# Leaving out, for the context tokens of a two-block transformer layer, the columns and results that only latent tokens use

## The chip, the cores and the metric

The kernel runs on one core of a Trainium2 chip. The number that counts is the device time of one execution in microseconds (us), the median over runs. Engines are called PE (TensorE matmul; PEld is its weight load), DVE (VectorE), ACT (ScalarE), POOL (GpSimd) and SP (SyncE, here a queue that only issues DMAs).

## The reference, cut to what matters

Two blocks run one after the other on 1,024 latent tokens of width 1,024. The change touches the first third of the first block, its token mix. That block has 256 context tokens beside the latent ones, but its depth is 1, so `need_ctx` is false and no output of a context token leaves it:

```python
u, uc = h @ w_in, hc @ w_in                     # 1024 and 256 tokens, 4544 columns
q, k, v, gf, gb = split_heads(u)                # retention, 5 x 512 columns
yc_f, sc_f = retention_scan(qc, kc, vc, log_gamma, s0)   # yc_f is not used, sc_f is
y_f, _ = retention_scan(q, k, v, log_gamma, sc_f)
r, w_f, w_b, k, v, a, b, g_f, g_b, bonus = rwkv_prepare(rw, ...)    # rwkv, 1984 columns
yc_f, sc_f = rwkv7_scan(rc, wc_f, kc, vc, ac, bc, s0)    # again only the state sc_f is used
y_f, _ = rwkv7_scan(r, w_f, k, v, a, b, sc_f)
if not need_ctx:
    return lat, None
```

The context serves for the two groups' states alone: of its retention part q and the two gates gf, gb are not used, and of its rwkv part the receptance r, the output gates and the per-token results.

## The kernel before

The program is a row of stages. Each stage is a block with its own buffers and semaphores, and the next begins when all engines and the queues of the last are done. Inside a stage every engine has its own written order of instructions with waits on semaphores; nothing is moved by a scheduler. Tokens stand context first: columns 0 to 255 of every transposed array are context (TC = 256), 256 to 1279 latent. P is 128, BANK is 512 columns of one PSUM bank.

**proj1** (`gemm_T`) writes `uT`, the 4,544 projected columns as rows, for 1,280 tokens. It has G = 18 groups of 256 columns (the last has 192). A group is two halves e of 128 columns (the last one 64), and each half three token chunks of 512, 512 and 256, each 8 x 3 matmuls (k tiles times hi x hi, lo x hi, hi x lo of a split product) into its own bank. ACT splits the next weights (`leading`, L527) and drains half 0 (L517); DVE makes the rest of the weights (`rest`, L548), drains half 1 (L517) and adds up the modulation vectors that later stages need (`piece`, L562); SP loads weights two groups ahead (L436), stores a half when it is drained (L468), and loads the pieces (L446).

**ret** (`retention`) loads q, k, v of 128 rows at a time (L665); only the latent part of q is read by any instruction. Its first work on DVE needs the table `ax`, loaded behind the first q and k.

**prep** (`rwkv_prepare`) goes over 12 units, four row pairs p times three token parts c: c = 0 is the 256 context tokens, c = 1 and 2 are 512 latent tokens each. In step i PE widens a norm for unit i - 3 (L1190), makes unit i's three convolutions k, v, r (`conv`, L1150), its low-rank products (L1164, L1166) and its norm sums (L1177), and for a latent unit i - 3 the gates (L1200) and the bonus sum (L1207). ACT takes the convolutions out of PSUM (L1254) between its exponentials (L1276 to L1278); DVE runs `rates`, `keys`, `results` of unit i - 3, the last of which multiplies r into one of four stored arrays (L1392, semaphore o1) and for latent units makes the bonus (L1397). POOL copies a few columns of the exponentials (`wcol`, L1125), for which L1392 waits, and after a context unit builds the nine diagonal matrices of the pair after next (L1103).

**chunks** (`rwkv_chunks`) takes 40 steps q, one for each pair and block of 128 tokens; 8 of them are context (the first two blocks of each pair's ten). A step inverts two triangular matrices by 5 levels of products in turn with ACT and DVE: `t1` on PE (L1541), a copy on ACT, `pp` on PE (L1551), a predicated copy on DVE (L1798). Between these PE does other work, among it for the step before: `results` (L1569, L1573, L1577; two blocks of 12 matmuls, in level 2 behind `pp` and in level 4 behind `t1`) and `states` (L1589 and on). DVE and ACT bring the results out (`res` L1811, `yis` L1711) beside the chunk matrices `mt`, `nn`. SP stores `res` and `yis` and loads the block four steps ahead, in a loop with registers. The next stage reads only the latent blocks of what was stored.

## Time and profile before

| | |
|---|---|
| median of 3 runs | 4752.97 us (4750.97 to 4757.22) |
| profiled execution, span | 4752.7 us |
| PE busy | 4004.5 us, 84% |
| DVE busy | 2760.1 us, 58% |
| ACT busy | 2047.4 us, 43% |
| stages that the change touches | 57 to 1500 us of the span |
| behind them, untouched | 1500 to 4752.7 us |

The profiled execution's own time is its span, 4752.7 us, 0.3 us under the median of the runs; a sum made in the span can be laid on the median as it is. A matmul record's length is pipelined (records overlap), so the time that a run of matmuls takes is read from start to start. Float32 matmuls stand in the trace as two records each, those on the split fp32r operands as one.

### The profile page before, as it was taken

To read this page: it belongs to the slowest core of one execution; us is meant where nothing else is said; L and a number is where in the kernel's file an instruction comes from. 1 tells how busy PE (TensorE), PEld (TensorE's weight loads), DVE (VectorE), ACT (ScalarE), POOL (GpSimd) and SP (SyncE) were. 2 spreads that over 40 slices of the span, in tenths; PEclk is the share of its full clock that TensorE was granted. 3 is DMA by queue.
4 is the path that set the end of the run, shared out by engine and by line. 5 is a ranking of instruction groups with operands and counts; after the bars stand their busy time and mean duration, and the time that the engine had idled before them with its cause. 6 is when DMAs were issued, how large, how long until landed. Compare 5 with 4: busy or idle time off the path is not lost. (4 is left out here: it accounts for less than half of the span.)

```text
span 4752.7 us, 76279 instructions
## 1 busy us (share of the span) xinstructions
PE 4004.5 (84%) x31217; PEld 3199.8 (67%) x31217; DVE 2760.1 (58%) x4042; ACT 2047.4 (43%) x3461; POOL 470.8 (10%) x376
## 2 busy tenths in 40 slices
PE   6999976878887675999939889699989896499994
PEld 4888744448886454888838767477777664388883
DVE  4222155566665558999951476455543354599995
ACT  3111022545553324777731344355532232377772
POOL 0000012210001200111010132000000000111111
PEclk9999966979999787999969999899999898699997
DMA  5332221652223445999942232322133304699996
GB/s 203 133 133 99 79 99 53 176 166 80 78 80 112 143 178 200 395 398 390 377 150 93 92 113 85 105 71 75 55 109 104 113 28 179 251 409 413 410 413 249
DMA packets 378959, 842.33 MB, mean 177 GB/s; under 512 B 32703, under 2 KB 249823, under 8 KB 328182
## 3 DMA queue, kind: packets, MB, share of 16 engines
q1 hardware_dynamic: 360526, 787.44, 45.2%
q0 software_dynamic: 12032, 41.96, 2.8%
q10 hardware_dynamic: 6056, 8.08, 0.5%
q8 instruction: 249, 4.08, 0.4%
q14 instruction: 96, 0.79, 0.1%
HBM read 673.03 MB, written 164.35 MB: 176 GB/s over the span
## 5 line engine op out<-in xcount | busy, mean ns | idle before, releaser
L506 PE MATMUL psum<-proj_hi,proj_w 128*128 128x512 f32 (+2 forms) x1728 | 461.8, 356 | 13.1 <-DVE proj_w L548 11.4
L4443 DVE TENSOR_TENSOR moe_lo<-moe_raw,moe_hi 128x2048 fp32r<-128x2048 f32 x192 | 428.4, 2286 | 33.6 <-ACT moe_hi L4398 33.6
L4398 ACT ACTIVATE moe_hi<-moe_raw 128x2048 fp32r<-128x2048 f32 x192 | 357.0, 1911 | 40.9 <-PE psum L4359 40.9
L506 PEld LDWEIGHTS psum<-proj_hi,proj_w 128*128 128x128 f32 (+1 forms) x1728 | 303.9, 188 | 66.6 <-DVE proj_w L548 11.6
L506 PE MATMUL psum<-proj_lo,proj_w 128*128 128x512 f32 (+2 forms) x864 | 306.2, 354 | 0.0
L517 DVE COPY proj_out<-psum 128x512 f32<-128x512 f32 (+3 forms) x54 | 32.5, 603 | 355.6 <-PE psum L506 355.6
L2738 DVE TENSOR_TENSOR moe_lo<-ahead_raw,moe_hi 128x2048 fp32r<-128x2048 f32 x96 | 219.1, 2290 | 23.5 <-ACT moe_hi L2686 23.4
L2738 DVE TENSOR_TENSOR moe_lo<-lT,moe_hi 128x2048 fp32r<-128x2048 f32 x96 | 218.9, 2290 | 21.9 <-ACT moe_hi L2686 21.9
L2686 ACT ACTIVATE moe_hi<-ahead_raw 128x2048 fp32r<-128x2048 f32 x96 | 184.2, 1919 | 70.9 <-PE psum L2639 70.9
L2686 ACT ACTIVATE moe_hi<-lT 128x2048 fp32r<-128x2048 f32 x96 | 183.9, 1919 | 66.3 <-PE psum L2639 66.3
L1798 DVE COPY_PREDICATED chunks_X<-chunks_msk,psum 128x128 f32<-128x128 int32 x400 | 107.8, 302 | 152.3 <-PE psum L1551 138.0
L1711 ACT ACTIVATE chunks_T<-psum 128x128 f32<-128x128 f32 x400 | 102.9, 278 | 206.3 <-PE psum L1541 202.0
L506 PEld LDWEIGHTS psum<-proj_lo,proj_w 128*128 128x128 f32 (+1 forms) x864 | 162.4, 188 | 23.9
L4359 PE MATMUL psum<-moe_hi,moe_xh 128*128 128x512 f32 x512 | 165.6, 405 | 9.8 <-DVE moe_lo L4443 9.8
L3387 PE MATMUL psum<-h_hi,g_w 128*128 128x512 f32 x512 | 169.1, 412 | 0.0
L506 PE MATMUL psum<-h_hi,proj_lru_w 128*128 128x512 f32 x512 | 159.2, 392 | 11.7 <-DVE proj_lru_w L548 11.7
L2639 PE MATMUL psum<-moe_hi,moe_xh 128*128 128x512 f32 x512 | 162.0, 398 | 4.9 <-DVE moe_lo L2738 4.9
L3487 DVE TENSOR_REDUCE attn_nmax<-psum 128x1 f32<-128x256 f32 (+7 forms) x128 | 90.9, 752 | 128.8 <-PE psum L3339 128.8
L4359 PE MATMUL psum<-moe_hi,moe_xl 128*128 128x512 f32 x512 | 160.5, 395 | 0.0
L4359 PE MATMUL psum<-moe_lo,moe_xh 128*128 128x512 f32 x512 | 159.7, 393 | 0.0
L2639 PE MATMUL psum<-moe_hi,moe_xl 128*128 128x512 f32 x512 | 159.1, 392 | 0.0
L2639 PE MATMUL psum<-moe_lo,moe_xh 128*128 128x512 f32 x512 | 159.0, 392 | 0.0
(647 smaller groups left out, 9940.2 us busy)
## 6 DMA issues: line engine op xcount, KB each, us to landing
moe_raw<-in_w_gate_up SPq DMA_DIRECT2D x128, 1024.0 KB, 9.6
moe_raw<-in_w_down SPq DMA_DIRECT2D x64, 1024.0 KB, 7.8
lT<-in_w_gate SPq DMA_DIRECT2D x36, 1024.0 KB, 9.3
ahead_raw<-in_w_down SPq DMA_DIRECT2D x36, 1024.0 KB, 8.0
ahead_raw<-in_w_up SPq DMA_DIRECT2D x32, 1024.0 KB, 10.1
lT<-in_w_up SPq DMA_DIRECT2D x32, 1024.0 KB, 9.7
ahead_raw<-in_w_gate SPq DMA_DIRECT2D x28, 1024.0 KB, 8.9
lT<-in_w_down SPq DMA_DIRECT2D x28, 1024.0 KB, 7.9
```

What stands on the lines that cost most here:

```text
L506: ins = nc.tensor.matmul(bank[e * nch + c][0:width, 0:n], l, r, start=(k == 0 and i == 0), stop=(k == KD - 1 and i == 2))
L517: ins = nc.scalar.activation(o, i, ACT.Copy) if e == 0 else nc.vector.tensor_copy(o, i)
L1711: nc.scalar.activation(dst, src, ACT.Copy).then_inc(s[sem], 1)
L1798: nc.vector.copy_predicated(X[:, j, g, :, c], msk[:, g, 1 + l, :, c], Lb[g][:, P:3 * P].rearrange("p (h t) -> p h t", h=2)[:, :, c])\
L2639: last = nc.tensor.matmul(out[c][:, :], x[:, k, :], w[:, n % R, i, c * BANK:(c + 1) * BANK], start=(k == 0 and m == 0), stop=(k == KD - 1 ...
L2686: nc.scalar.activation(hi[:, n % R], raw(n), ACT.Copy).then_inc(s["hi_ready"], 1)
L2738: nc.vector.tensor_tensor(lo[:, n % R], raw(n), hi[:, n % R], ALU.subtract).then_inc(s["lo_ready"], 1)
L3387: ins = nc.tensor.matmul(bank[7][:, :], g_w[:, c % 2, l, k, :], h_part[r][:, k, b * BANK:(b + 1) * BANK], start=(k == 0 and i == 0), stop= ...
L3487: nc.vector.tensor_reduce(nmax[:, j, m:m + 1], psum[:, at(j, m):at(j, m) + n], AX_X, ALU.max, negate=True)\
L4359: last = nc.tensor.matmul(out[c][:, :], x[:, k, :], w[:, n % R, i, c * BANK:(c + 1) * BANK], start=(k == 0 and m == 0), stop=(k == last_k ...
L4398: nc.scalar.activation(hi[:, n % R], raw[:, n % RAW], ACT.Copy).then_inc(s["hi_ready"], 1)
L4443: nc.vector.tensor_tensor(lo[:, n % R], raw[:, n % RAW], hi[:, n % R], ALU.subtract).then_inc(s["lo_ready"], 1)
```

## The change

In the projection nine of the 18 groups start at token 256 (`NO_CONTEXT`): groups 0, 1 (retention q), 6 to 9 (retention gates), 10, 11 (r) and 17 (the tail of the output gates' low-rank columns). They have two token chunks of 512 instead of three; every count of semaphores goes by `before[g]`, the chunks of the groups ahead. The retention stage loads q from column 256. In prep a context unit loads no r, has no r convolution, no copy of it and no product o1 (the bare exponential is stored in its place, and is not used); the waits that hung on these go by the latent units alone. In chunks a context step has no `results` matmuls, no `res` and `yis`, and no stores, and SP's loop is written out.

```diff
+NO_CONTEXT = (0, 1, 6, 7, 8, 9, 10, 11, 17)
...
+    begin = [TC if g in late else 0 for g in range(G)]
+    chunks = [[(a, min(BANK, tok - a)) for a in range(begin[g], tok, BANK)] for g in range(G)]
+    before = [sum(len(chunks[j]) for j in range(g)) for g in range(G + 1)]
...
-                        sp.wait_ge(ev[e], nch * (g + 1))
-                        sp.dma_start(dst[g * GW + e * P:g * GW + e * P + size[g][e], :], ob[0:size[g][e], e, :]).then_inc(stored[e], 16)
+                        sp.wait_ge(ev[e], before[g + 1])
+                        sp.dma_start(dst[g * GW + e * P:g * GW + e * P + size[g][e], begin[g]:tok], ob[0:size[g][e], e, begin[g]:tok])\
+                            .then_inc(stored[e], 16)
...
-                            pe.wait_ge(ev[e], nch * g)
+                            pe.wait_ge(ev[e], before[g])
                         width = size[g][e]
-                        for c, (a, n) in enumerate(chunks):
+                        for c, (a, n) in enumerate(chunks[g]):
...
-                        sp.dma_start(t[:, b, :], uT[p * P + a:p * P + a + P, :]).then_inc(loaded[b], 16)
+                        first = TC if t is q else 0
+                        sp.dma_start(t[:, b, first:], uT[p * P + a:p * P + a + P, first:]).then_inc(loaded[b], 16)
...
+        def streams(n):
+            return "kvr" if latent(n) else "kv"
...
-                    for k in range(2):
+                    for k in range(0 if latent(n) else 1, 2):
...
-                        sp.wait_ge(done, n + 1)
+                        if done is s["o1"]:
+                            sp.wait_ge(s["exps"], 3 * n + 3)
+                            sp.wait_ge(done, lat(n + 1))
+                        else:
+                            sp.wait_ge(done, n + 1)
...
-                    for which in "kvr":
+                    for which in streams(n):
...
-                        act.wait_ge(s["o1"], n - R + 1)
+                        act.wait_ge(s["o3"], n - R + 1)
+                        act.wait_ge(s["o1"], lat(n - R + 1))
...
-                        conv_out(i, "r")
+                        if latent(i):
+                            conv_out(i, "r")
...
-                    nc.vector.tensor_tensor(e[:, 0, :, 0:m], e[:, 0, :, 0:m], both(un[:, 0, 0:m]), ALU.mult).then_inc(s["o1"], 1)
+                    if latent(n):
+                        dve.wait_ge(s["ring_ev"], ring_at["r", n] + 1)
+                        nc.vector.tensor_tensor(e[:, 0, :, 0:m], e[:, 0, :, 0:m], both(un[:, 0, 0:m]), ALU.mult).then_inc(s["o1"], 1)
...
+        def latent(q):
+            return q % NBK >= NTC
...
-                    sp.sem_inc(s["turns"], 1)
-                    for dst, src in ((re, res), (yi, yis)):
+                    for dst, src in ((re, res), (yi, yis)) if latent(q) else ():
...
-                with sp.Fori(0, Q // R - 1) as it:
-                    for j in range(R):
-                        store(it * R + j)
-                        load(it * R + (R + j), j)
+                for q in range(Q):
+                    store(q)
+                    if q + R < Q:
+                        load(q + R)
...
+                    if not latent(q):
+                        return
                     four(out_a)
                     four(out_v)
                     four(out_v2)
...
-                        nc.vector.tensor_tensor(res[:, :, c, :], b[:, 0], pr[:, j, 1:4:2, half[c]], ALU.add).then_inc(s["c_dve"], 1)
+                        if latent(q):
+                            nc.vector.tensor_tensor(res[:, :, c, :], b[:, 0], pr[:, j, 1:4:2, half[c]], ALU.add).then_inc(s["c_dve"], 1)
```

Nothing is put in another order; instructions fall out of the engines' orders. In chunks, this is PE's order in step 1, from `pp` of level 2 to `pp` of level 3 (L1541 is `t1`, L1551 and L1553 `pp`, L1512 and L1514 the transposes of the step after, L1569 to L1577 `results` of step 0, a context block). Before:

```order
L1551 MATMUL psum<-chunks_T,chunks_X 64x64 x8
L1569 MATMUL psum<-chunks_LL,chunks_TT 64x64 x4
L1573 MATMUL psum<-chunks_LL,chunks_TT 64x64 x4
L1577 MATMUL psum<-chunks_LL,chunks_vrow 64x64 x4
L1541 MATMUL psum<-chunks_X,chunks_LL 64x64 x8
L1512 MATMUL psum<-cst,chunks_pr 128x128 x3
L1514 MATMUL psum<-cst,chunks_vt 128x128
L1512 MATMUL psum<-cst,chunks_pr 128x128 x3
L1551 MATMUL psum<-chunks_T,chunks_X 64x64 x8
```

And in the changed kernel (L1579 is `pp`, L1569 now `t1`, L1540 and L1542 the transposes):

```order
L1579 MATMUL psum<-chunks_T,chunks_X 64x64 x8
L1569 MATMUL psum<-chunks_X,chunks_LL 64x64 x8
L1540 MATMUL psum<-cst,chunks_pr 128x128 x3
L1542 MATMUL psum<-cst,chunks_vt 128x128
L1540 MATMUL psum<-cst,chunks_pr 128x128 x3
L1579 MATMUL psum<-chunks_T,chunks_X 64x64 x8
```

The 12 matmuls of `results` between `pp` and `t1` are gone; the second 12, between `t1` and `pp` of level 4, go in the same way.

In prep, this is PE's order around the second context convolution (unit 3), before:

```order
L1190 MATMUL psum<-prep_rs,prep_spread 128x128 x2
L1150 MATMUL psum<-prep_rin,prep_dg 128x256 x9
L1164 MATMUL psum<-prep_wl,prep_w2t 128x256 x2
L1166 MATMUL psum<-prep_al,prep_a2t 128x256
L1177 MATMUL psum<-prep_sqk,prep_zsel 32x128 x2
L1190 MATMUL psum<-prep_rs,prep_spread 128x128 x4
L1150 MATMUL psum<-prep_rin,prep_dg 128x512 x9
```

And in the changed kernel:

```order
L1209 MATMUL psum<-prep_rs,prep_spread 128x128 x2
L1169 MATMUL psum<-prep_rin,prep_dg 128x256 x6
L1183 MATMUL psum<-prep_wl,prep_w2t 128x256 x2
L1185 MATMUL psum<-prep_al,prep_a2t 128x256
L1196 MATMUL psum<-prep_sqk,prep_zsel 32x128 x2
L1209 MATMUL psum<-prep_rs,prep_spread 128x128 x4
L1169 MATMUL psum<-prep_rin,prep_dg 128x512 x9
```

The context convolution has six matmuls for nine, and everything behind it on PE stands as before.

## Rows read from the trace of the kernel before

**Rows 1.** The page's first line and its engines.

```profile
span 4752.7 us, 76279 instructions
```

**Rows 2.** Busy time by window: us; PE, PEld, DVE, ACT, POOL; clock, DMA.

```profile
57.00:582.00 525.00, 508.22 (x2614) 427.32 (x2612) 133.04 (x130) 73.36 (x85) 0.00 (x0) 0.99 0.33 112
582.00:811.00 229.00, 170.54 (x1200) 110.02 (x1200) 114.23 (x248) 60.05 (x163) 29.85 (x12) 0.68 0.20 72
811.00:1027.00 216.00, 162.46 (x496) 85.30 (x496) 142.40 (x186) 111.49 (x174) 62.59 (x82) 0.83 0.67 191
1027.00:1500.00 473.00, 407.40 (x13080) 386.81 (x13080) 285.22 (x1120) 231.62 (x999) 41.53 (x40) 0.97 0.29 79
```

**Rows 3.** Waits, window 57 to 585: total us, times, longest.

```profile
DVE proj_out L517 <- PE psum L506: 355.6, 54, 18.9
```

**Rows 4.** Timeline of PE, group 0: start us, us, what.

```profile
85.02 0.40 PE L506 MATMUL psum<-proj_hi,proj_w 128*128 128x256 f32 x2
87.89 0.63 PE L506 MATMUL psum<-proj_hi,proj_w 128*128 128x512 f32 x2
```

**Rows 5.** Timelines of ACT and SP, groups 7, 8; landings of proj_raw.

```profile
298.86 1.92 ACT L527 ACTIVATE proj_w<-proj_raw 128x2048 fp32r<-128x2048 f32 x1 [13.46 <-PE psum L506]
326.41 1.91 ACT L527 ACTIVATE proj_w<-proj_raw 128x2048 fp32r<-128x2048 f32 x1 [13.45 <-PE psum L506]
...
308.81 0.38 SPq L436 DMA_DIRECT2D proj_raw<-in_w_in  x1
...
DMA to landing us min/median/max: 5.3/7.2/11.0
```

**Rows 6.** Tile ret_q; timeline of DVE at the start of ret.

```profile
L665 SPq DMA_DIRECT2D ret_q<-uT x4: 319/324/432, 582.6 to 695.8; - x4
...
591.74 0.69 DVE L886 TENSOR_TENSOR ret_tmp<-psum,ret_ax 128x512 f32<-128x512 f32 x1 [12.94 <-DMA ret_ax<-in_ax]
```

**Rows 7.** Timeline of PE in prep, steps 6 and 7; one window.

```profile
904.51 6.54 PE L1150 MATMUL psum<-prep_rin,prep_dg 128*128 128x256 f32 x18
913.68 8.00 PE L1150 MATMUL psum<-prep_rin,prep_dg 128*128 128x512 f32 x18
...
905.00:910.00 5.00, 5.00 (x14) 3.96 (x14) 0.77 (x3) 0.95 (x3) 0.00 (x0) 0.56 0.45 142
```

**Rows 8.** Timelines of PE and ACT at the start of prep.

```profile
825.67 6.70 PE L1150 MATMUL psum<-prep_rin,prep_dg 128*128 128x256 f32 x18 [17.70 <-POOL prep_dg L1103]
...
830.36 1.28 ACT L1298 ACTIVATE prep_wl<-prep_wl 128x1282 f32<-128x1282 f32 x1 [24.57 <-issue]
```

**Rows 9.** Timelines of DVE and POOL in prep, units 3, 4 and 7.

```profile
914.27 0.78 DVE L1392 TENSOR_TENSOR prep_ex<-prep_ex,prep_u 128x512 f32<-128x512 f32 x1
926.30 1.22 DVE L1392 TENSOR_TENSOR prep_ex<-prep_ex,prep_u 128x1024 f32<-128x1024 f32 x1 [0.77 <-POOL wcol L1125]
971.45 0.69 DVE L1397 TENSOR_TENSOR prep_gt<-psum,prep_u 128x512 f32<-128x512 f32 x1 [0.88 <-PE psum L1207]
...
914.14 11.78 POOL L1103 TENSOR_SCALAR prep_dg<-cst,prep_pcs 128x128 f32<-128x128 f32 x9
```

**Rows 10.** Timeline of PE in chunks, step 0.

```profile
1047.22 0.63 PE L1551 MATMUL psum<-chunks_T,chunks_X 64*64 64x64 f32 x16
1048.02 0.68 PE L1541 MATMUL psum<-chunks_X,chunks_LL 64*64 64x64 f32 x16 [0.17 <-DVE chunks_X L1798]
1050.40 0.68 PE L1541 MATMUL psum<-chunks_X,chunks_LL 64*64 64x64 f32 x16 [0.17 <-DVE chunks_X L1798]
1051.22 0.68 PE L1553 MATMUL psum<-chunks_X,chunks_T 64*64 64x64 f32 x16
```

**Rows 11.** Timeline of PE in chunks, a later step.

```profile
1128.90 0.34 PE L1597 MATMUL psum<-chunks_vrow,chunks_rows 64*64 64x64 f32 x7 [1.67 <-issue]
1133.90 0.56 PE L1551 MATMUL psum<-chunks_T,chunks_X 64*64 64x64 f32 x13
1134.74 0.68 PE L1541 MATMUL psum<-chunks_X,chunks_LL 64*64 64x64 f32 x16
```

More of the change, by code:

```diff
@@ L396, in turn, with gemm_T @@
         return (KD * v + KD - 1) // self.PER + 2
-def gemm_T(nc, bank, name, actT, tok, w, col0, widths, dst, later=None, split=None):
+def gemm_T(nc, bank, name, actT, tok, w, col0, widths, dst, later=None, split=None, late=()):
     full, last = widths
-    chunks = [(a, min(BANK, tok - a)) for a in range(0, tok, BANK)]
-    nch = len(chunks)
+    nch = (tok + BANK - 1) // BANK
     GW = 2 * P
@@ L513, in drain @@
                 width = size[g][e]
-                for c, (a, n) in enumerate(chunks):
-                    eng.wait_ge(mm[e], g * nch + c + 1)
+                for c, (a, n) in enumerate(chunks[g]):
+                    eng.wait_ge(mm[e], before[g] + c + 1)
                     o, i = ob[0:width, e, a:a + n], bank[e * nch + c][0:width, 0:n]
@@ L525, in leading @@
                     if g >= 2:
-                        act.wait_ge(mm[1], nch * (g - 1))
+                        act.wait_ge(mm[1], before[g - 1])
                     nc.scalar.activation(wt[:, g % 2, 0, :, 0:n], raw[:, g % 2, :, 0:n], ACT.Copy).then_inc(hi_ready, 1)
@@ L546, in rest @@
                     if g >= 2:
-                        dve.wait_ge(mm[1], nch * (g - 1))
+                        dve.wait_ge(mm[1], before[g - 1])
                     nc.vector.tensor_tensor(wt[:, g % 2, 1, :, 0:n], raw[:, g % 2, :, 0:n], wt[:, g % 2, 0, :, 0:n], ALU.subtract)\
@@ L1039, in pc @@
             return pcs[:, p, PCOL[name] + i:PCOL[name] + i + 1]
+        def streams(n):
+            return "kvr" if latent(n) else "kv"
         ring_at = {}
         for n in range(STEPS):
-            for k in range(3 if n < UNITS else 0):
-                ring_at["kvr"[k], n] = len(ring_at)
+            for which in streams(n) if n < UNITS else "":
+                ring_at[which, n] = len(ring_at)
             for d in range(2 if n >= NP and latent(n - NP) else 0):
@@ L1088, in _ @@
                     if n < UNITS - NP:
-                        sp.wait_ge(s["ring_mm"], ring_at["r", n] + 1)
+                        sp.wait_ge(s["ring_mm"], ring_at[streams(n)[-1], n] + 1)
                         load_unit(n + NP)
@@ L1141, in conv @@
                     p, c, a, m = unit(n)
-                    pe.wait_ge(rin_in[c], 64 * (p + 1))
+                    pe.wait_ge(rin_in[c], (64 if latent(n) else 48) * (p + 1))
                     if n == 0:
@@ L1439, in rwkv_chunks @@
         names = ("tab_in", "tr", "rows_ev", "g_mm", "ll", "x_id", "x_one", "x_tr", "lakv_mm", "lakv_ev", "t1_mm", "t1_ev",
-                 "p_mm", "x_ev", "x_turned", "ta_mm", "ta_ev", "y_mm", "c_dve", "c_act", "stored", "turns")
+                 "p_mm", "x_ev", "x_turned", "ta_mm", "ta_ev", "y_mm", "c_dve", "c_act", "stored")
         s = {n: st.sem(n) for n in names}
@@ L1447, in rwkv_chunks @@
         PER_IN = 16 * 2
+        def latent(q):
+            return q % NBK >= NTC
+        c_dve = [sum(4 if latent(t) else 2 for t in range(q)) for q in range(Q + 1)]
+        c_act = [sum(6 if latent(t) else 4 for t in range(q)) for q in range(Q + 1)]
+        stored = [sum(32 if latent(t) else 0 for t in range(q)) for q in range(Q + 1)]
         def each_step(step):
@@ L1668, in out0 @@
                             if evac:
-                                after("c_act", q * 6 - 6)
+                                after("c_act", c_act[q - 1])
                             results(q - 1, jp, 0)
@@ L1738, in out @@
                 def out(q, j, c):
-                    act.wait_ge(s["c_dve"], q * 4 + (2 * c + 2))
-                    if c == 0:
-                        act.wait_ge(s["stored"], q * 32 + 1)
-                    copy(yis[:, :, c, :], Cb[c][:, P:2 * P].rearrange("p (d t) -> p d t", d=2), "c_act")
+                    act.wait_ge(s["c_dve"], c_dve[q] + (c + 1) * (2 if latent(q) else 1))
+                    if latent(q):
+                        if c == 0 and stored[q]:
+                            act.wait_ge(s["stored"], stored[q])
+                        copy(yis[:, :, c, :], Cb[c][:, P:2 * P].rearrange("p (d t) -> p d t", d=2), "c_act")
                     for d in range(2):
@@ L1807, in out @@
                     dve.wait_ge(s["y_mm"], q + 1)
-                    dve.wait_ge(s["stored"], q * 32 + 1)
+                    if latent(q) and stored[q]:
+                        dve.wait_ge(s["stored"], stored[q])
                     for c in range(2):
                         b = Cb[c][:, :].rearrange("p (w d t) -> p w d t", w=4, d=2)
-                        nc.vector.tensor_tensor(res[:, :, c, :], b[:, 0], pr[:, j, 1:4:2, half[c]], ALU.add).then_inc(s["c_dve"], 1)
+                        if latent(q):
+                            nc.vector.tensor_tensor(res[:, :, c, :], b[:, 0], pr[:, j, 1:4:2, half[c]], ALU.add).then_inc(s["c_dve"], 1)
                         nc.vector.tensor_tensor(mt[:, :, 2 * (q % NBK) + c, q // NBK, :], b[:, 2], idc.unsqueeze(1).to_broadcast([P, 2, H]), ALU.add)\
@@ L4554, in program @@
                 [(cst[:, :], tabs["cst"]), (col[:, :], tabs["cols"])], sc, x["ctx"][0], x["x"][0], hT)
-        gemm_T(nc, bank, "proj1", hT, TT, x["w_in"][0], 0, (D_IN // 512 * 2, ((P, P), (P, 64))), uT,
+        gemm_T(nc, bank, "proj1", hT, TT, x["w_in"][0], 0, (D_IN // 512 * 2, ((P, P), (P, 64))), uT, late=NO_CONTEXT,
                later=Later(x["w_mod"], x["b_mod"], x["norm_gains"], sc, cst[:, CONST["ones"]:CONST["ones"] + 1], mod))
```

22 lines of the change are left out of this document (10 added, 12 removed).

## The prediction

> **What bounds the kernel now.** I read the span cut at the stages first. The profiled execution took 4752.7 us [rows 1]; the change touches four stages, from 57 to 1500 us, and what lies behind is not edited. The reader is to see in the windows that each stage has a limit of its own: in proj1 PE is busy 508 of 525 us, at a granted clock of 0.99 of full speed (the 2.4 GHz level); in ret and prep PE's clock is at 0.68 and 0.83 and no engine is full; in chunks PE is busy 407 of 473 us [rows 2].
>
> For proj1 the view of waits comes next. DVE waits there for PE before all of its 54 drains, 356 us in all [rows 3], and ACT waits 13.5 us for it before each weight split [rows 5]. So the stage is PE's matmuls, one behind the other, and a matmul left out is time won as long as weights and drains keep up.
>
> For ret I read what its first DVE work waits for: the table `ax` [rows 6]. For prep and chunks the shares of busy time say little, since engines wait for each other by turns; there I went through the timelines of all engines over one pair and over one step, and asked at each removed instruction which wait ends last behind it.
>
> **proj1.** In group 0, the 24 matmuls of 128x256 of one half run from 85.02 to 87.89, 2.87 us [rows 4]; the next half's 512-wide ones begin at once. A late group loses two such chunks, 5.74 us, and there are nine late groups: 9 x 5.74 = 51.7. Against it goes that the last half has 64 weight columns, so that its chunk may be a little shorter, and that the last drain before the stage's end is now 512 wide instead of 256; 0.4 us for both is an estimate. I take **-51.3**.
>
> Do weights keep up? The load for group 10 is issued at 308.81 and lands 7.2 us later in the median, 11.0 at worst, while ACT can't begin to split before group 8 ends, at 326.41 [rows 5]. That leaves 10.4 us, 6.6 at worst; a late group takes 5.74 of it. Even a load behind that would have a whole group more, since group 9 runs in between. DVE has 356 / 54 = 6.6 us to spare before each drain, its splits, pieces and sums included [rows 3]. So nothing new is waited for; this term's bounds are -50 and -52.
>
> **ret.** q, k and `ax` are 640, 640 and 1024 KB, issued from 582.6, and DVE starts when `ax` has landed at 591.74 [rows 6]: 2304 KB in 9.1 us, 0.5 us for the 128 KB that q loses. Later loads are early. **-0.4**, bounds 0 and -0.6.
>
> **prep.** A context unit loses 3 of 9 convolution matmuls on PE, one copy on ACT and one product on DVE. On PE, 18 records of 512 take 8.00 us at the high level, 0.444 each, so six of 256 are 1.33 us; the nine of a context unit took 6.54, as they begin behind a wait with the clock at 0.56, and a third of that is 2.18 [rows 7]. The r matmuls are the last three, when the clock has risen, so I take 1.33. On DVE L1392 costs 0.6 to 0.7 us of its queue [rows 9]. Whether that counts must be asked for each of the four context units:
>
> - Start: PE runs units 0 to 2 without a gap and DVE waits for the end of that. But behind the shorter convolution PE needs the tanh that ACT ends at 830.36 + 1.28 = 831.64 [rows 8], and 825.67 + 6.70 - 1.33 is 831.04. So 0.7 to 0.8 of the 1.33 is had.
> - Pairs 0 and 1: DVE comes 0.7 us sooner to the next unit, and at its L1392 waits for `wcol`, which POOL copies behind nine diagonals that start at 914.14 and take 11.78, to 925.9 [rows 9]. These start by ACT's exponentials, which the change doesn't move. The gain ends there: 0.
> - Pair 2 (no diagonals follow): DVE waits 0.88 us at L1397 for PE's bonus sum [rows 9]. DVE's 0.7 and PE's 1.33 both come through: 1.3.
> - Pair 3: DVE runs on without a wait, 0.6.
>
> Sum **-2.7**. Bounds: 0, and 4 x (1.33 + 0.6) = -7.7 if both engines' savings added up each time.
>
> **chunks.** Eight context steps lose twice 12 matmuls (24 records). Do these cost time? In a later step the block between `pp` and `t1` is there, and `t1` starts 0.84 us behind `pp` (1133.90 to 1134.74) [rows 11]. Step 0 has no results before it, so the same place is empty: 1047.22 to 1048.02 is 0.80, with 0.17 of it idle for the DVE copy. The place between `t1` and `pp` of level 4 takes 0.82 there (1050.40 to 1051.22) [rows 10]. The block fills the time of DVE's or ACT's answer. That makes 0.04 and about 0.02 a step, 0.5 us for eight.
>
> There is a second cost: PE stops now and then for nothing that the profile shows, as 1.67 us at 1128.90 [rows 11]. In the window PE is idle at most 473 - 407 = 66 us, start and end of the stage included [rows 2], and a large part of that are such stops. If they come by the number of instructions fed, 8 x 48 of 13,080 records is 2.9% of them, 1.4 us. The `res` and `yis` instructions lie in idle time of DVE and ACT; DVE's block at a step's start ends before `pp` asks. The written-out queue on SP issues four blocks ahead and hides. **-1.9**, bounds 0 (both for nothing) and -7.5 (each 24-record block at 0.38 us, 6.1, and the 1.4).
>
> TensorE: Matmul & The Clock Gate, section "Wait — 56ns, not 53.3ns?", of the Trainium skill says that matmuls never start closer than about 25 ns however narrow. By it the 384 records would be an estimated 9.6 us. The pair of places above, with and without the block, doesn't show it.
>
> **Sum.** -51.3 - 0.4 - 2.7 - 1.9 = -56.3, against the execution's own 4752.7: 4696.4. The median of the runs lies 0.3 above it, so 4696.7.
>
> **Rivals.**
>
> *Feeding PE is the limit in chunks and prep.* PE is 86% busy in chunks, which speaks for it. Then each block returns 0.38 us and each context unit 1.9 in prep: -51.3 - 0.4 - 7.7 - 7.5 = -66.9, 4686. Against it stand the two equal places of step 0 and the idle 0.17. Somewhere halfway, 4687 to 4691, is more likely than the full case. By the skill's rule the time would be 2 us less again. Chance 0.12.
>
> *The late groups are bound by something else.* If group 8's load lands at its worst, and a store or piece load on SP delays its issue by 5 us more, the split comes late; it costs only what is over a whole group of 21.8 us. (A group takes 326.41 - 298.86 = 27.55 now [rows 5].) To lose 10 us of the 51, four of nine groups would have to wait 2.5. No wait of PE is of this kind now. This also takes in stops of PE elsewhere that fall otherwise in the changed program: 4704 to 4720. Chance 0.08.
>
> *The gain is not there at all*, within 9.5 us of before: every late group would have to be held within 1 us of its old 27.55 by weights or drains. Chance 0.02.
>
> *Slower.* One mechanism could do it: chunks has 40 steps, and SP's queue is now written out, without the loop. If its instructions came so slowly that a block's load or the store before it were late, PE or DVE would wait in each step. It decides at 56 / 40 = 1.4 us a step; at 1.7 us it is 68 - 56 = 12 us slower, 4765. That a step has four DMAs at most in about 11 us, and that blocks are loaded four steps ahead, speaks against it. Chance 0.02.
>
> **How the numbers follow.** The forecast as summed, 4691 to 4703, has 0.76. Its range comes from the terms' bounds: proj1 by 1.3, prep and chunks by halves of theirs. The whole range goes on to 4688 below, where the first rival's halfway case lies, and to 4704 above. A measurement of this kernel tells about 0.2%, 9.5 us, from no change. Faster by more than that: forecast, first rival and most of the second, 0.96; same 0.02; slower 0.02.
>
> **What would show it.** Late groups spaced 21.8 us and the others 27.5, with ACT and DVE still waiting for PE; the 128x256 matmuls down from 864 to 432. In prep, context units' convolutions of about 5.2 us, `wcol` still held behind the diagonals in pairs 0 and 1, and the wait at L1397 gone in pair 2; the stage 2 to 3 us shorter. In chunks, context steps within 0.2 us of the latent ones, stops aside. Stage lengths then: proj1 474, ret 229, prep 213, chunks 471. It is wrong if a late group is over 23 us, if chunks gives 5 us or more, or if the stages behind 1500, which nobody edited, change by more than 3 us in all.

## The result

The changed kernel takes 4678.45 us (median of 4 runs, 4673.49 to 4695.68) beside 4755.1 of the kernel before in the same session: ratio 0.9848, 95% interval 0.9831 to 0.9864. It is faster, as forecast, but by 76.6 us where 56 were forecast, and below the range (4688 to 4704). Four more runs of it in another session (e4) gave 4687.13 (4682.03 to 4691.52) beside 4756.06, that is 68.9 us less, ratio 0.9858 (0.9833 to 0.9883). So the size of the gain is known to some 8 us. One execution of run e15, 5420.5 us at a granted clock of 0.716, is in a slower state and is left out everywhere below.

The page of the changed kernel, for [rows 1]; the second line is an engine's busy time, share and instructions:

```profile
span 4676.1 us, 74178 instructions
...
PE 3935.4 (84%) x30377; PEld 3129.9 (67%) x30377; DVE 2750.4 (59%) x4013; ACT 2038.5 (44%) x3432; POOL 469.5 (10%) x376
...
q1 hardware_dynamic: 355598, 781.99, 45.8%
...
q8 instruction: 243, 3.98, 0.4%
```

The windows, cut at the same instruction of each stage in every profile (the first load of weights, of q and of the convolutions' input, the first load of v in chunks, and DVE's first instruction of the stage behind), for [rows 2]; the columns are length, then busy time and instructions of PE, PEld, DVE, ACT, POOL, then granted clock, DMA share and GB/s:

```profile
58.40:529.80 471.40, 456.03 (x2176) 375.02 (x2176) 127.21 (x114) 68.29 (x71) 0.00 (x0) 0.98 0.35 120
529.80:753.30 223.50, 164.91 (x1200) 106.99 (x1200) 114.48 (x248) 59.86 (x163) 29.82 (x12) 0.71 0.20 71
753.30:968.80 215.50, 157.03 (x472) 79.33 (x472) 139.76 (x181) 110.38 (x170) 62.05 (x82) 0.84 0.66 190
968.80:1426.10 457.30, 399.22 (x12717) 378.10 (x12719) 281.97 (x1104) 229.07 (x984) 41.46 (x40) 0.98 0.28 78
1426.10:4676.10 3250.00, 2724.98 (x13658) 2173.88 (x13655) 2059.41 (x2286) 1542.26 (x1971) 335.92 (x238) 0.91 0.55 207
```

The same cuts in the profile of before give the table's first column; the reader is to see that proj1 came as forecast, and that ret and chunks did not:

| stage | before | after | difference | forecast |
|---|---|---|---|---|
| proj1 (first instruction to ret's first load) | 523.3 | 471.4 | -51.9 | -51.3 |
| ret | 229.4 | 223.5 | -5.9 | -0.4 |
| prep | 216.9 | 215.5 | -1.4 | -2.7 |
| chunks | 475.6 | 457.3 | -18.3 | -1.9 |
| ahead and behind | 3307.5 | 3308.4 | +0.9 | 0 |

The last row, which nobody edited, is 3301.8 to 3312.4 in all 17 profiles, so one pair of profiles can't be read closer than that as a whole.

In proj1, ACT's weight splits in its timeline, for [rows 5]: two late groups, then two of those with the context.

```profile
320.41 1.92 ACT L536 ACTIVATE proj_w<-proj_raw 128x2048 fp32r<-128x2048 f32 x1 [10.34 <-PE psum L515]
342.17 1.92 ACT L536 ACTIVATE proj_w<-proj_raw 128x2048 fp32r<-128x2048 f32 x1 [10.34 <-PE psum L515]
363.93 1.91 ACT L536 ACTIVATE proj_w<-proj_raw 128x2048 fp32r<-128x2048 f32 x1 [10.34 <-PE psum L515]
...
421.10 1.92 ACT L536 ACTIVATE proj_w<-proj_raw 128x2048 fp32r<-128x2048 f32 x1 [13.46 <-PE psum L515]
448.66 1.92 ACT L536 ACTIVATE proj_w<-proj_raw 128x2048 fp32r<-128x2048 f32 x1 [13.46 <-PE psum L515]
```

A late group takes 21.76 us and one with the context 27.56 (21.8 and 27.5 forecast), and ACT still waits 10.3 us for PE. DVE waits for PE before all of its 45 drains, 310.0 us in all, in the view of waits, for [rows 3]:

```profile
DVE proj_out L526 <- PE psum L515: 310.0, 45, 17.1
```

**What the stops in chunks are.** In PE's timelines of chunks the stops that nothing in the profile explains ("issue", as in [rows 11]) stand at the same matmuls in two executions of one program. Four of them in the changed kernel:

```profile
1032.41 0.39 PE L1569 MATMUL psum<-chunks_X,chunks_LL 64*64 64x64 f32 x6 [1.59 <-issue]
1054.06 0.27 PE L1619 MATMUL psum<-chunks_rows,chunks_TT 64*64 64x64 f32 x1 [1.22 <-issue]
1074.88 0.33 PE L1605 MATMUL psum<-chunks_LL,chunks_vrow 64*64 64x64 f32 x3 [1.05 <-issue]
1087.39 0.57 PE L1569 MATMUL psum<-chunks_X,chunks_LL 64*64 64x64 f32 x10 [1.46 <-issue]
```

and of the same kernel in run e4:

```profile
1033.68 0.39 PE L1569 MATMUL psum<-chunks_X,chunks_LL 64*64 64x64 f32 x6 [1.72 <-issue]
1055.61 0.27 PE L1619 MATMUL psum<-chunks_rows,chunks_TT 64*64 64x64 f32 x1 [1.23 <-issue]
1076.04 0.33 PE L1605 MATMUL psum<-chunks_LL,chunks_vrow 64*64 64x64 f32 x3 [1.05 <-issue]
1088.78 0.57 PE L1569 MATMUL psum<-chunks_X,chunks_LL 64*64 64x64 f32 x10 [1.70 <-issue]
```

So they hang on the place in the program. I counted PE's instructions in the trace in their order (weight loads, matmuls, semaphore instructions). A gap is here the time from a matmul's start to the next one's. Of the changed kernel's 41 gaps over 0.5 us in chunks, 39 stand at the same place modulo 256 (within two), and of the 43 of before 41. The instruction queue q8 moves packets of 16,384 bytes, one for 256 of PE's instructions: 243 for 30377 x 2 matmuls and weight loads and some 1,100 semaphore instructions. From this count and the times below I take a stop to be PE waiting for its next block of instructions; e8 below tests it. The transfers of all kinds around the first stop above, in 40 slices from 1022 to 1034 us, and SP's timeline beside it:

```profile
GB/s 0 0 0 0 0 0 0 0 55 0 0 80 278 75 19 271 150 133 164 36 157 346 352 350 321 162 0 0 0 0 0 0 0 0 0 0 0 0 55 0
...
q1 hardware_dynamic: 1728, 0.85, 25.1%
q8 instruction: 3, 0.05, 1.7%
```

```profile
1024.59 0.37 SPq L1500 DMA_DIRECT2D re<-chunks_res  x1
1025.00 0.94 SPq L1500 DMA_DIRECT2D yi<-chunks_yis  x1
1025.98 0.48 SPq L1493 DMA_DIRECT2D chunks_pr<-prim  x1
1026.50 0.66 SPq L1494 DMA_DIRECT2D chunks_vt<-vT  x1
```

Three instruction blocks move in 12 us. Two stand alone as "55", at 1024.66 and 1033.61 by their packet records. The third begins as the last of the step's 1,728 other packets end (1029.79), runs from 1029.75 to 1030.88, and PE goes on at 1032.41. Over the steps PE comes back 1.2 to 1.7 us behind the block's end wherever it had stopped. From PE's crossing of one such place to the next block's start it takes 1.3 us in the mean where PE isn't stopped by that block, and 2.1 to 2.2 where it is; PE needs mostly 3.5 to 4 us for 256 instructions when it runs on. Of the 97 such places in the changed kernel's steps, 36 have other packets on over 30% of the DMA engines' time from 1 us before the block's start to its end, and their gap is 0.97 us in the mean; the 34 with no other packet in that time have 0.20.

Where the Trainium skill (Runtime: NRT & Kernel Launch, "Instruction fetch mechanics") says that PE's instructions come in blocks of 16 KiB, 256 instructions, this trace agrees. It calls the cost of crossing from one block to the next "mostly hidden". Here it is not: 43.7 us of the changed kernel's steps and 54.9 of before's are gaps over 0.5 us at these places.

### The profile page after: what moved, and what is told of

It is laid out like the page before. It is cut to its first block and busy times, and to the rows that moved or that the text cites. A ratio compares the mean times of both kernels' runs of the same rounds, so it can differ in the third digit from the quotient of the medians.

```text
span 4676.1 us, 74178 instructions
## 1 busy us (share of the span) xinstructions
PE 3935.4 (84%) x30377; PEld 3129.9 (67%) x30377; DVE 2750.4 (59%) x4013; ACT 2038.5 (44%) x3432; POOL 469.5 (10%) x376
## 5 line engine op out<-in xcount | busy, mean ns | idle before, releaser
L515 PE MATMUL psum<-proj_hi,proj_w 128*128 128x512 f32 (+2 forms) x1440 | 410.0, 370 | 12.9 <-DVE proj_w L557 11.3
L515 PEld LDWEIGHTS psum<-proj_hi,proj_w 128*128 128x128 f32 (+1 forms) x1440 | 259.4, 188 | 66.1 <-DVE proj_w L557 11.7
L515 PE MATMUL psum<-proj_lo,proj_w 128*128 128x512 f32 (+2 forms) x720 | 265.6, 369 | 0.0
L526 DVE COPY proj_out<-psum 128x512 f32<-128x512 f32 (+2 forms) x45 | 28.7, 638 | 310.0 <-PE psum L515 310.0
L2959 PE MATMUL psum<-qkv_w_hi,h_hi 128*128 128x512 f32 x384 | 126.3, 411 | 30.9 <-DVE qkv_w_lo L3127 26.4
```

Source lines behind the costliest of these rows:

```text
L515: ins = nc.tensor.matmul(bank[e * nch + c][0:width, 0:n], l, r, start=(k == 0 and i == 0), stop=(k == KD - 1 and i == 2))
L2959: last = nc.tensor.matmul(bank[2 * (n % 2) + c_][:, :], l_[:, k, i * P:(i + 1) * P], r_[:, k, c_ * BANK:(c_ + 1) * BANK], start=(k == 0 an ...
```

## The experiments

Chunks is given as its stage's length, and as the 39 steps between the first and the last of the 40 marks that DVE sets, one a step; "stops" are the gaps over 0.5 us at the 256th instructions between these marks. "Low" is the time between the same marks in which PE's clock was granted at the 1.2 GHz level. "Place" says by how many instructions PE's stream in chunks is moved against before, modulo 256. "Late" is by how much the steps began later than in before. Each row is one profile.

| run | place | chunks | 39 steps | first step | stops | low |
|---|---|---|---|---|---|---|
| before | 0 | 475.6 | 439.3 | 9.5 | 54.9 | 13.8 |
| e13, before again | 0 | 472.4 | 436.4 | 9.5 | 53.2 | 13.6 |
| e2, queue written out | 0 | 474.7 | 439.3 | 9.5 | 56.7 | 13.6 |
| e7, moved | 56 | 470.5 | 434.8 | 9.4 | 50.2 | 13.3 |
| e9, moved | 111 | 473.0 (2.8 late) | 435.2 | 9.8 | 50.7 | 14.3 |
| e1, front half | 111 | 468.0 | 433.1 | 7.9 | 49.5 | 5.4 |
| e10, front half moved back | 0 | 473.0 (5.7 late) | 434.4 | 7.9 | 53.5 | 5.0 |
| e14, the same with matmuls | 1 | 479.4 | 443.0 | 7.9 | 58.1 | 15.6 |
| e3, chunks half | 0 | 465.0 | 429.7 | 9.6 | 40.5 | 20.7 |
| after | 111 | 457.3 | 422.4 | 7.9 | 43.7 | 1.6 |
| e4, after again | 111 | 459.3 | 424.3 | 7.9 | 45.0 | 5.5 |
| e5, stores back | 111 | 460.1 | 425.5 | 7.9 | 45.1 | 5.4 |
| e12, after moved | 239 | 469.8 (4.7 late) | 429.2 | 9.4 | 43.3 | 16.4 |
| e6, matmuls back | 111 | 468.5 | 432.0 | 7.9 | 52.7 | 4.6 |
| e11, narrow matmuls back | 111 | 466.5 | 431.9 | 7.9 | 50.2 | 8.6 |
| e8, blocks of 4 KB | 111 | 448.1 | 413.9 | 9.4 | 32.6 | 9.8 |
| e15, e8 with matmuls back | 111 | 453.2 | 418.9 | 9.4 | 35.6 | 9.4 |

**e1 to e4: which half, SP's loop, the spread.** e1 is before with the diff's hunks of proj1, ret and prep, e3 with those of chunks, e2 with SP's queue alone:

```diff
-                with sp.Fori(0, Q // R - 1) as it:
-                    for j in range(R):
-                        store(it * R + j)
-                        load(it * R + (R + j), j)
-                for j in range(R):
-                    store(Q - R + j)
+                for q in range(Q):
+                    store(q)
+                    if q + R < Q:
+                        load(q + R)
```

> The kernel before with the change in proj1, ret and prep alone; chunks as before, loop and all context results in it. Theory A (the surplus over the forecast lies in chunks, 18 us, and in ret, 6 us, each from its own edit or place): about 4755 - 52 - 6 - 1.5 = 4695, with chunks at 475 as in the kernel before. Theory B (the stops of PE in chunks fall by chance with the program's layout or the run): chunks may come out anywhere from 457 to 478 though nothing in it is edited. On ret: theory R1 (q's shorter load and no other cause) gives a ret stage 0.5 us shorter than before; theory R2 (the phases of PE's granted clock fall otherwise behind a shorter proj1) gives 5 us or more with the first load's gain of 1 us in it.

> The kernel before with SP's queue in chunks written out and nothing else: all results computed, drained and stored for the context too. Theory S (SP's loop with registers cost PE's instruction supply or delayed the blocks): chunks falls from 475 to 460 or less and the time by 10 us or more, to 4743. Theory P (the gain is in the context steps' missing matmuls and drains): chunks stays at 475, time 4755. The price that I gave the written-out queue was nothing.

> The kernel before with the change in chunks alone: proj1, ret and prep as before. Theory A (the gain belongs to the edit of chunks): chunks 457, time 4755 - 18 = 4737. Theory B (stops by chance of layout or of the run): chunks between 457 and 475, 4737 to 4753. By my forecast's price (1.9 us) it would be 4753. In ret nothing is edited: 229 by either theory.

> The changed kernel again, for the spread of its runs and of its stages. If the stages' lengths belong to the program, chunks is 457 within 2 us and ret 223.5 within 1; if they vary by run, either moves by 5 us or more. Time 4678 as before, 4695 in the odd run.

e1: 4690.76 us, ratio 0.9864 (0.9839 to 0.9889). e2: 4752.44, ratio 0.9989 (0.9975 to 1.0002). e3: 4739.44, ratio 0.9968 (0.9958 to 0.9979). Chunks in e1, where nothing of it is edited (13,102 matmul records as before), and in e3:

```profile
967.50:1435.50 468.00, 405.90 (x13102) 385.02 (x13103) 284.90 (x1120) 231.83 (x1000) 41.53 (x40) 0.98 0.29 80
```

```profile
1023.80:1488.80 465.00, 408.46 (x12718) 386.54 (x12720) 282.44 (x1105) 229.48 (x984) 41.53 (x40) 0.96 0.28 76
```

The written-out queue is worth nothing (474.7), as forecast. Against 472.4 to 475.6 of the three profiles at before's program (e13 below), the chunks half gives 7 to 11 us by itself, and the front half 4 to 8 in a stage that it doesn't edit. 1.6 of the latter are the first step, which spends 2.0 us at the 1.2 GHz level in e1 (7.95 us long) and 6.8 and 7.0 in e2 and e3 (9.46, 9.58). The front half doesn't give this for sure: e8, e12 and e15 have it in and a first step of 9.4. Ret is the other finding: unedited, it took 229.4 us in the profile of before but this in e2:

```profile
582.80:801.00 218.20, 158.63 (x1200) 103.88 (x1200) 114.51 (x248) 59.81 (x163) 29.84 (x12) 0.76 0.21 76
```

and this, with the shorter load of q, in e14:

```profile
530.40:759.80 229.40, 170.88 (x1200) 110.33 (x1200) 114.52 (x248) 60.03 (x163) 29.89 (x12) 0.68 0.20 70
```

Same instructions, DVE and ACT busy for the same time; the clock is 0.76 in the one and 0.68 in the other. By the clock's record ret ran 147 of 229.4 us at the 1.2 GHz level in before, 105 of 218.2 in e2, 128 of 223.5 in the changed kernel (the 143 and 99 in an expectation below are some 5 us low). Six profiles with the old ret span 218.2 to 229.6 (mean 226), eleven with the new one 219.4 to 229.4 (mean 224). The mean difference of 2 us can't be told from that spread, and R2's price of 5 us doesn't belong to the change. The start of the stage can be told: DVE's first product with `ax` begins 8.6 to 9.2 us behind the first load in the six old ones and 7.9 to 8.3 in the eleven new ones, 0.9 us sooner in the mean. That is the load of q alone, theory R1, at twice its price.

**e5, e6, e11: stores or instructions.** e5 stores a table where the context's results were stored, e6 drops the early return in `results`, e11 does it too but makes the context's products 8 columns wide. The results of e6 and e11 are not copied out. The edit of e11:

```diff
                 def results(q, j, d):
                     o = d * H
+                    n = H if latent(q) else 8
...
-                        nc.tensor.matmul(Cb[c][half[h], o:o + H], TT_[half[c], d, h, 0, :], LL[half[c], j, h, d, 0, 1, :],
+                        nc.tensor.matmul(Cb[c][half[h], o:o + n], TT_[half[c], d, h, 0, :], LL[half[c], j, h, d, 0, 1, 0:n],
...
-                    if not latent(q):
-                        return
```

> The changed kernel with the context steps' 16 stores in chunks back (a constant table is stored in the place of the results, which nothing reads); PE, DVE and ACT as in the changed kernel. The traces so far show that nearly every stop of PE over 0.5 us in chunks stands at the same place of its instruction stream, once in 256 instructions, behind a 16 KB packet of the instruction queue, and that the stops are longer (1.0 against 0.3 us) where other packets are in flight. Theory D (the stores' packets delay these transfers): chunks is 4 to 8 us longer than 457 to 459, 463 or more, and the time 5 us or more longer. Theory I (the gain is in PE's instructions that aren't there): chunks stays within 2 us of 458.

> The changed kernel with the context steps' results matmuls in chunks back (two blocks of 12, 24 records each, in eight steps); their results are neither copied out nor stored. Theory I (every instruction that PE is fed costs time here, since 256 instructions take PE hardly longer than their transfer): 8 x 48 records x 2 = 768 instructions, three transfers of 256 at 4.0 to 4.5 us each spread over the steps, chunks 6 to 12 us longer, 465 to 470. Theory D (the stores made the difference): chunks within 2 us of 458. By my forecast's price for the same matmuls it would be 1.9 us.

> The changed kernel with as many matmuls as the context's results had, but 8 columns wide instead of 64, not copied out nor stored. Instructions as with the matmuls back (768 more), array work an eighth. Theory F (the instructions cost their transfer, whatever they compute): chunks 467 to 469, as with the 64 columns (468.5). Theory W (it was the matmuls' own time on the array): 458 to 460, near the changed kernel's 457.3 and 459.3.

e5: 4688.41 us, ratio 0.9874 (0.9857 to 0.9891). e6: 4688.24, 0.9872 (0.9853 to 0.9891). e11: 4686.77, 0.9862 (0.9846 to 0.9879). The medians don't tell them from e4; the stage does. Chunks of e6, and of e11:

```profile
970.70:1439.20 468.50, 404.20 (x13102) 384.52 (x13104) 281.74 (x1104) 229.18 (x984) 41.46 (x40) 0.98 0.27 76
```

```profile
965.30:1431.80 466.50, 404.80 (x13102) 385.11 (x13104) 281.68 (x1104) 229.38 (x984) 41.45 (x40) 0.98 0.27 76
```

The 16 stores are worth nothing beyond the spread (460.1 against 457.3 and 459.3): theory D fell. The 384 records cost 7.9 us of steps in e6 (432.0 against 424.1, the mean of after, e4 and e5) and 7.8 in e11 with an eighth of the columns: it is the instructions, not what they compute (one profile each, where three of the same PE stream span 3.1 us). The profile says where. In the view of PE's waits over chunks the first rows of the changed kernel and of e6 are

```profile
PE psum L1569 <- issue: 9.3, 11, 2.0
```

```profile
PE psum L1569 <- issue: 15.1, 16, 2.0
```

(us in all, times, longest), the same line of `t1`, which e6 doesn't touch. Stops over 0.5 us go from 44.6 in the mean of the three to 52.7 and 50.2. What is left of the steps without the stops is 379.2 us in e6, against 378.7 to 380.4 in the three: outside the stops these 384 records cost nothing there. In e11 it is 381.7, with 8.6 us at the low level instead of 1.6 to 5.5.

**e7, e9, e10, e12, e14: the place in the stream.** Waits that are already met, two to an instruction, stand at the start of PE's stream in chunks; in e14 one-column matmuls. The edit of e9:

```diff
+                pe.sem_inc(s["pad"], 1)
+                for _ in range(220):
+                    pe.wait_ge(s["pad"], 1)
                 pe.wait_ge(s_in[0], PER_IN)
```

> The kernel before with 111 waits that are already met put at the start of PE's stream in chunks, where PE waits 19.8 us for its first block anyway. This moves PE's stream by as many instructions against the multiples of 256 as the front half of the change did (145 fewer of 256 is 111 more). Theory L (where the 256th instruction falls in a step decides its stop): the steps come out as in the kernel with the front half alone, context steps 82 to 84 us in all instead of 90.6 and 88.0, chunks 468 to 470. Theory C (that gain was the granted clock at the stage's start): the context steps stay at 88 to 91 us and chunks at 475 or a little more.

> The kernel before with PE's stream in chunks moved by 111 instructions against the multiples of 256: 221 waits that are already met stand at the start of the stage, where PE waits for its first block (two of them make one instruction, so that the 111 waits of the run before this one moved it by 56, and chunks was 470.5). The stops then fall in the places of a step where the kernel with the front half alone has them. Theory L (the place of the 256th instruction decides): chunks 468 to 471, steps like that kernel's but for the first, which that kernel does 1.6 us faster by the granted clock. Theory C (the front half's 7.6 us in chunks were the clock and the run): 474 to 476.

> The kernel with the front half of the change alone, PE's stream in chunks moved by 145 instructions, so that the stops fall where the kernel before has them. The reverse of the run above. Theory L: chunks 473 to 475 instead of 468, that is 475 less the first step's 1.6, and the time 5 to 7 us longer, about 4696. Theory C: chunks stays at 468.

> The changed kernel with PE's stream in chunks moved by 128 instructions, half a block, in the same way as the runs above. How much of the changed kernel's chunks (457.3 and 459.3) is where the stops happen to fall. Theory L: anywhere from 455 to 465, other steps stopped than now, and the same stops in each run. Theory C: 457 to 460, the same steps as now.

> The kernel with the front half of the change alone, PE's stream in chunks moved by 145 instructions again, now by 36 matmuls of one column (four instructions each) in place of the waits, which took 0.11 us each and made the stage start 5.7 us late. Theory L (the stops fall by their place in the stream): the 39 steps take 437 to 439 us in all, as in the kernel before less the first step's 1.6, and chunks is 473. Otherwise, as the run with the waits gave (434.4): 433 to 435 and chunks 468; then the place in the stream is not the whole of what the front half changed in chunks.

e7 4754.98 us, ratio 0.9998 (0.9987 to 1.0009); e9 4753.08, 1.0 (0.999 to 1.001); e10 4697.26, 0.9889 (0.9869 to 0.991); e12 4687.94, 0.9868 (0.9851 to 0.9884); e14 4691.36, 0.988 (0.9863 to 0.9896). In stops the place shows both ways: 53.2 to 58.1 us in the five profiles at place 0 or 1 with all matmuls in, 49.5 to 50.7 at 56 and 111. Which steps are long goes with the place too, in both directions: over the 38 steps behind the first, the lengths in e9 correlate with e1's at 0.69 and with before's at -0.28, and those of e10 and e14 with before's at 0.68 and 0.62 and with e1's at -0.16 and -0.08. In e9 the steps behind the first two of each pair take 351.2 us in all, as in e1 (351.1) and not as in before (348.7), and the first two 84.0 and 82.0 instead of 90.6. In the steps' sum it holds in one direction (e7, e9: 435 against 436.4 to 439.3), but e10 stayed at 434.4, below the 437 expected, and e14 overshot with 443.0 in a profile that was the slowest of its four executions (4709.6 against 4689.3 to 4693.3). So the place decides which steps are stopped and is worth about 4 us of stops; for the steps' sum the reverse test is inconclusive, and no median shows it.

The column of low clock tells what hides it. e14 has 4.6 us more of stops than e10, and 15.6 us at the low level instead of 5.0; its steps without the stops are 384.9 us against 380.9. These 4.6 and 4.0 are the 8.6 between them. e12's stops are as the changed kernel's, but its steps without them are 385.9 us instead of 378.7 to 380.4, with 16.4 us at the low level instead of 1.6 to 5.5; that is where its 5 to 7 us more lie, 1.5 of them in the first step. No run sets the clock by itself, so this is read from the profiles and not tested.

**e8, e15: the other transfers.** `prim` is laid out by row, so that a block is read in 4 KB pieces:

```diff
-    prim, vT = scratch("prim", Q, 8, P, P), scratch("vT", Q, P, P)
+    prim, vT = scratch("prim", Q, P, 8, P), scratch("vT", Q, P, P)
...
-                            sp.dma_start(prim[b, at[d]].rearrange("b c t -> c b t"), src[:, d, 0:m].rearrange("p (b t) -> p b t", t=P))\
+                            sp.dma_start(prim[b, :, at[d]].rearrange("b c t -> c b t"), src[:, d, 0:m].rearrange("p (b t) -> p b t", t=P))\
...
-                    sp.dma_start(pr[:, j], prim[q].rearrange("n c t -> c n t")).then_inc(s_in[j], 16)
+                    sp.dma_start(pr[:, j], prim[q]).then_inc(s_in[j], 16)
```

> The changed kernel with the blocks that chunks loads laid out by row, so that a block's load reads 4 KB in one piece for each of the 128 rows instead of eight pieces of 512 bytes. Same bytes, PE, DVE and ACT untouched; prep stores pieces of 512 bytes as now. If the load's many packets are what delays PE's instruction transfers, the stops beside a load shrink from 1.0 us towards 0.3 and chunks falls from 458 by 5 to 20 us, the time to 4660 to 4675. If the delay goes by bytes or has another cause, chunks stays within 2 us.

> The kernel whose blocks are loaded in pieces of 4 KB, with the context's results matmuls back. Theory F with the other transfers in the way (an instruction costs time only where its transfer is late): fewer late transfers, so less than the 9 us that the same matmuls cost without that layout: chunks 448 + 4 to 8 = 452 to 456. If instructions cost their price by number alone, independent of the other transfers: 457 or more.

> The kernel before once more, one profile. With unedited proj1 and ret, ret was 229.4, 218.2, 220.1, 229.6 and 229.0 in five profiles so far. If ret's length follows the moment at which the granted clock falls and rises in it, it is again one of these, 218 to 230, by the low-clock time in it (99 us in the shortest, 143 in the longest). If it belongs to the program, it is 229. Chunks: 473 to 477 by either.

e8: 4674.29 us (4668.33 to 4680.62), ratio 0.9838 (0.9821 to 0.9855), the fastest version here, though its interval overlaps that of the changed kernel; that of e5, run beside it, lies above (0.9857 to 0.9891). Its page and its chunks:

```profile
q1 hardware_dynamic: 319758, 781.99, 45.5%
```

```profile
972.20:1420.30 448.10, 400.41 (x12718) 380.38 (x12720) 281.91 (x1104) 229.46 (x984) 41.45 (x40) 0.97 0.26 79
```

35,840 packets fewer for the same bytes, PE's busy time as before it (400 us), and 9 to 12 us gone from the stage: stops 32.6 instead of 44.6. Blocks that come among other packets, counted as above, have gaps of 0.71 us instead of 0.97. e15 (4675.16 us, ratio 0.9836, 0.9816 to 0.9857) puts the results matmuls back on that: chunks 453.2, 5.0 us of steps instead of 7.9, and 3.0 of stops instead of 8.1. That speaks for a price that hangs on how late the blocks come, but 2.9 us between single profiles is no more than the spread of 3.1, so it isn't shown. e13 took 4745.7 us in its one execution, beside 4747.45 of the same kernel's others; it had ret 229.1 and chunks 472.4, a little under the 473 expected. So two profiles of one program agree in ret (229.4 and 229.1 here, 223.5 and 224.5 in the changed kernel), and it is programs with the same ret that differ, by up to 11 us. Whether that belongs to the program or to the execution stays open: e2's profile, with 218.2, was also the fastest of its ten executions (4741.75 us against a median of 4752.44).

## Why the prediction missed

- **proj1** was right: -51.9 for -51.3, at the same spacing, with nothing new waited for.
- **ret** had the mechanism right and the size not: the first product with `ax` comes 0.9 us sooner, where 0.5 and in sum 0.4 were forecast. The rest of the -5.9 between the two profiles goes with the time at the low clock (147 and 128 us) and is inside the spread of unedited rets.
- **prep** came near in its sum by luck. The means of six old and eleven new profiles, 218.6 and 215.7, give -2.9 for -2.7, but the old ones span 215.8 to 220.8 by when the first convolution begins. Compared with its like (e13 and e4, both 15.7 us into the stage) it is -2.0, and not by the forecast's terms. From one bonus product of DVE to the next, the start gains 1.1 us (0.75 forecast), pair 1 0.4 (0), pair 2 2.7 (1.3) and pair 3 1.1 (0.6), 5.3 in all; two latent stretches lose 1.7 each. Every profile with the new prep has two latent convolutions of 9.6 to 9.7 us, and none with the old has one over 8.0. The second latent convolution of pair 1, as windows of before and of the changed kernel (the clock is the third number from the end):

```profile
929.30:937.30 8.00, 8.00 (x21) 3.40 (x20) 6.46 (x9) 3.73 (x6) 0.00 (x0) 1.00 1.03 296
871.50:881.10 9.60, 9.60 (x21) 4.09 (x22) 6.41 (x9) 3.76 (x6) 0.00 (x0) 0.83 0.81 245
```

So PE's granted clock falls in two latent convolutions in all eleven profiles with the shorter context convolution and in no latent one of the six others, and no term of the forecast had this. The convolutions of the context themselves are 5.42 and 5.47 us at the start and in pair 1 (5.2 forecast), 4.4 and 4.5 in pairs 2 and 3; the wait for the bonus sum in pair 2 fell from 0.88 to 0.16.
- **chunks** is the step that failed, with -1.9 for 8 to 9 us that the matmuls cost: 7.9 and 7.8 in e6 and e11, 8.6 in e3 against the mean of before, e13 and e2. Most of it is in the term for the stops. The forecast had "8 x 48 of 13,080 records is 2.9% of them", 1.4 us. The count of blocks does go by it (104 to 101), but the stops grew by 8.1 us in e6 and 5.6 in e11, and by 3.0 in e15; they fell by a quarter from before to e3 (54.9 to 40.5), since another stream also changes which blocks are late. The other term, "The block fills the time of DVE's or ACT's answer", 0.5 us, was read from step 0, whose places of [rows 10] have no stop in them. Outside the stops it held in e6 (-0.3 us); in e11 and e15 2.0 to 2.2 us are left, and 4.2 from e1 to the mean of after, e4 and e5, so it is not shown to hold in general.
- **The front half's effect on chunks** had no term at all: 1.6 us for the first step, most of which is at the high clock, and about 4 for the place in the stream. Another 1 us lies at the stage's end (the last mark to the next stage, 25.2 to 26.2 us in before, e13 and e2, 24.5 to 24.9 in after, e4 and e5); it isn't tied to either half, since e1 has 25.0, e3 25.2 and e14 26.3.

By means of three profiles each (before, e13, e2 against after, e4, e5) chunks fell by 474.2 - 458.9 = 15.3 us. Cut by halves, e3 gives 9.2 of it and e1 6.1. Cut by kind, 10.3 are stops, 3.9 the rest of the steps, which had 4.2 us at the low level instead of 13.7, and 1.0 the stage's end. By causes, 8 for the matmuls, 4 for the place, 1.6 for the first step and 1 at the end make 14.6; the 4 is the least certain of them. The other 3 of the pair's 18.3 are spread between executions.

The first rival, feeding PE as the limit, was the right one for chunks, with a price of 7.5 that was 0.5 to 1.5 short (its 0.38 us a block stood in no row; e6 gives 0.49, stops included), and too high for prep; I held it at 0.12 because of two places without a stop. The rule of the Trainium skill that the prediction cites (TensorE: Matmul & The Clock Gate, "Wait — 56ns, not 53.3ns?"), that matmuls never start closer than about 25 ns, gave an estimated 9.6 us, near the size. That e11 costs the same fits it too. But in [rows 11] the 40 records from 1133.90 to 1134.74 (16 of `pp`, 24 of results) begin 21 ns apart in the mean, and in e6 the added time is all in the stops, so the blocks are the better account. By the forecast's own sign, chunks over 5 us meant it was wrong, and it was. Its other sign, 3 us in the stages that nobody edited, was too narrow: they span 10.6 us over these profiles.

Open: what makes the granted clock fall in some steps of one profile and not of another (e10 and e14), what part of the 8 to 9 us is stops, and what sets the moment at which a block's transfer begins.

## What to carry to other kernels

Where an engine runs many small instructions, look at its unexplained stops by their count of instructions, not by time: if they recur each 256, it is fed by transfers, and what counts is the number of instructions and the packets in their way. Leaving instructions out then can pay more than their own time, and larger pieces for the other transfers pay without touching the engine (e8). Before a difference in a stage that nobody edited is explained, profile other programs with the same stage: ret moved by 11 us between them, with 42 us more at the low clock. And when work is taken from PE in a stage whose clock is not steady, look at the granted clock behind it: in prep that gave back 3.4 of 5.3 us.

## What the hardware showed that I had not expected

- PE's instructions arrive in packets of 16 KB, 256 instructions, 1.1 to 1.2 us each in the mean in chunks; PE restarts 1.2 to 1.7 us behind the end of one it waits for.
- An instruction of two waits that are already met costs 0.106 us on PE. In e10 they took 16.0 us from the stage's start to its first matmul, which otherwise comes at 9.3, and the steps began 5.7 us late.
- Matmuls of 8 columns cost as much as of 64 here (431.9 and 432.0 us of steps, one profile each).
- A convolution of 8.0 us took 9.6 to 9.7 where the clock fell in it, twice in each of the eleven profiles with the shorter context convolutions, and never in the six with the longer ones.
